# Second block of a two-block transformer on one core: 36 of 44 slabs of each large stage read normed, shifted rows; ScalarE evicts; modulation loads and small exchanges move to POOL's queue

## The chip, the cores and the metric

The kernel runs on one NeuronCore of one Trainium2 chip. Its engines work side by side: TensorE (PE) multiplies, and loads its weights in a stream of its own (PEld); VectorE (DVE), ScalarE (ACT) and GpSimd (POOL) compute on rows; SyncE (SP) issues DMA transfers, and so can ACT and POOL, each from its own queue. The 16 DMA engines are shared. Engines meet only at semaphores. The metric is the device time of one launch in microseconds (us): 1425.88 us is the median of three runs of the kernel before (1425.37 to 1426.09).

## The reference, cut to what matters

Input x has 256 tokens of width 1024. First come two hybrid layers (attention, mLSTM, MLP), which the change touches only through their DMA queues. Then two layers of the second block:

```python
mod = silu(c) @ w_ada[l] + b_ada[l]                       # (1024) x (1024, 6144)
sh1, sc1, g1, sh2, sc2, g2 = split(mod, 6)
h = rmsnorm(x, norm1[l]) * (1 + sc1) + sh1
proj = h @ w_in[l]                                        # (256, 1024) x (1024, 5632)
q, k, v, g_sw, p_in, gates = split(proj)                  # q, k: rotary; retention; pooling
merged = sigmoid(a_ret) * (... @ w_ret_o[l]) + sigmoid(a_pool) * (... @ w_pool_o[l])
x = x + g1 * (merged @ w_out[l])
h2 = rmsnorm(x, norm2[l]) * (1 + sc2) + sh2
gate, up = split(h2 @ w_ffn_in[l], 2)                     # (256, 1024) x (1024, 5632)
x = x + g2 * ((silu(gate) * up) @ w_ffn_out[l])
```

rmsnorm divides each token's row by its root mean square. The modulation vector mod is one matrix-vector product per layer, from 24 MB of weights.

## The kernel before, in words

**Slabs.** Every weight matrix is cut into slabs of 1024 x 128 values (512 KB), 450 in all. A slab passes through four steps, always in the same order: SP loads it into one of NS = 8 places of `raw`, once the slab eight before it has been used (`slab_used`); ACT copies it to `w_hi` (L583), rounded to the type that TensorE multiplies fast; DVE writes the rest, `w_lo` = raw - w_hi (L1082); PE multiplies. Activations are split in the same way, into a high and a low part. The function `slab` (L1938 to L1940) makes 24 matmuls of a slab: for each of its eight row tiles k, high by high, high by low and low by high. A slab's result, 128 features by 256 tokens, gathers in one of four banks of `acc`, so that a bank is written again four slabs later.

**Stages of the second block.** Slabs 190 to 319 are its first layer, 320 to 449 its second. In each: 44 slabs of w_in (I call it the projection stage), 8 of w_ret_o, 4 of w_pool_o, 8 of w_out, 44 of w_ffn_in, alternately gate and up (u counts the 22 pairs), and 22 of w_ffn_out. The first w_ffn_in slab of layer 0 is slab 254.

**The norm is folded in behind the matmul.** The rows `h2` that the projection and w_ffn_in stages multiply are x times the column gain, not yet divided by the root mean square, so that PE can start before that root is known. After the 256 token columns stand two more columns that hold the shift (high and low part); a matmul here therefore moves W = 258 columns. When a slab is done, DVE multiplies 258 columns of the bank by `rstd` (in `to_sbuf`, L1600, and for gate and up at L1874 and L1877; `rstd` has ones in its last columns), and the shift's product is added as a bias afterwards: by ACT in `shift` (L909) in the projection stage, within silu (L1052) and within the product of gate and up (L1881) in the other.

**Order of work.** It is written out by hand for each engine. `hi_upto(i)` and `lo_upto(i)` on ACT and DVE make all parts up to slab i. A queue is strictly in order: what stands behind a waiting instruction waits too.

**Modulation.** `load_ada` on SP loads `ada`, 96 pieces of 512 KB, into three places; DVE multiplies and adds them (`ada_product`, L1166 and L1172, two per piece), PE sums them (`ada_sums`, L1990) and DVE takes the columns (`ada_columns`). SP's queue holds these loads between those of the slabs; a load of `ada` waits for the place to be free (`ada_sum`), and the slab loads stand behind it.

**Rotary.** q and k are exchanged by halves of a head through SBUF-to-SBUF DMAs (`partners`, four DMAs of 64 KB each, into `rotb`), also on SP; `rope2` on DVE waits for them.

**The names in the order's rows.** `hn_x`, `hn_hi` and `hn_lo` are new semaphores: a pair of tiles of x times rstd is ready, a high tile is ready, a low pair is ready. `landed3` and the like are the landings of a raw place.

## Time and profile before

| | |
|---|---|
| median of 3 runs | 1425.88 us |
| the profiled execution, its own time | 1428.8 us |
| its span (first to last instruction) | 1426.1 us |
| mean granted TensorE clock | 0.996 |
| PE / PEld / DVE / ACT / POOL busy | 98 / 92 / 80 / 58 / 1 % |
| DMA queues | SP and its like 292.00 MB (72.9% of 16 engines' span); POOL's 1.66 MB |

Busy is a share of the span. All times of a trace count from the start of the span. A row of the timeline has start, duration, engine, line, operation, output<-inputs and shape; "x3" joins three instructions, and what stands in brackets is the idle time before it and what ended it. Instructions of one engine overlap a little: the step from one start to the next is shorter than the duration. In a row of the stretches, the numbers behind the length are the busy time of each engine with its count of instructions, then the granted TensorE clock (1.00 is 2.4 GHz, 0.50 is 1.2 GHz), the busy share of the DMA engines and GB/s.

### The profile page before, as it was taken

The numbers are of one execution on the slowest core, as the hardware profiler recorded it, in microseconds if no ns is written. First come the engines' busy times: TensorE is split into PE (matmuls) and PEld (weight loads), VectorE is DVE, ScalarE is ACT, GpSimd is POOL, SyncE is SP. The second block draws the span as 40 slices with busy tenths as digits, with TensorE's granted clock in tenths as the row PEclk, the third lists the DMA queues.
The fourth block names the chain that finished last, engine by engine and source line by source line (L and its number), as shares of the span: only waits on it lengthen the run. The fifth ranks groups of instructions, "written<-read, shape, count | busy, mean of one in ns | idle before, by whom it ended". The sixth has DMA issues, their size and how long they took to land.

```text
span 1426.1 us, 25528 instructions
## 1 busy us (share of the span) xinstructions
PE 1401.7 (98%) x10325; PEld 1312.9 (92%) x10325; DVE 1147.6 (80%) x1805; ACT 822.8 (58%) x1245; POOL 10.5 (1%) x21
## 2 busy tenths in 40 slices
PE   8999999999999999999999999999999999999997
PEld 8898888888888888889999999998999999999986
DVE  7898888888898888887778777777787887777763
ACT  6776776445776775344656555444446575644552
POOL 2000000000000000000000000000000000000000
PEclk9999999999999999999999999999999999999998
DMA  9544999986446999988754578898787556778661
GB/s 263 157 143 117 285 265 272 292 226 163 134 140 191 272 263 297 278 245 225 213 148 148 176 235 224 220 252 227 231 230 217 147 151 184 228 208 235 179 186 65
DMA packets 485363, 297.12 MB, mean 208 GB/s; under 512 B 14956, under 2 KB 455792, under 8 KB 485120
## 3 DMA queue, kind: packets, MB, share of 16 engines
q1 hardware_dynamic: 483728, 292.00, 72.9%
q8 instruction: 82, 1.34, 0.4%
q10 hardware_dynamic: 816, 1.84, 0.4%
q0 software_dynamic: 704, 1.66, 0.3%
q14 instruction: 33, 0.27, 0.1%
HBM read 289.43 MB, written 1.05 MB: 204 GB/s over the span
## 4 chain that ended last, share of the span: by engine, by line
PE 78%; DVE 13%; issue 3%; ACT 3%; DMA 2%; SPq 1%; DVEq 0%; ACTq 0%
PE acc L1938 15%; PE acc L1939 15%; PE acc L1940 14%; PE acc L1955 8%; PE mx L1955 6%; DVE w_lo L1082 5%; PE acc L1956 4%; PE mx L1956 3%; DVE ada_acc L1172 3%; ACT w_hi L583 1%; PE acc L1970 1%; PE acc L1972 1%; PE acc L1971 1%; DMA raw<-in_w_down 1%; DMA rotb<-projb 1%
## 5 line engine op out<-in xcount | busy, mean ns | idle before, releaser
L1082 DVE TENSOR_TENSOR w_lo<-raw,w_hi 128x1024 fp32r<-128x1024 f32 x450 | 541.6, 1221 | 111.2 <-ACT w_hi L583 109.4
L583 ACT ACTIVATE w_hi<-raw 128x1024 fp32r<-128x1024 f32 x450 | 458.0, 1049 | 135.5 <-DMA raw<-in_w_in 82.5
L1938 PE MATMUL acc<-h,w_hi 128*128 128x258 f32 (+1 forms) x1776 | 509.4, 287 | 7.6 <-DVE h L1109 2.8
L1939 PE MATMUL acc<-h,w_hi 128*128 128x258 f32 (+1 forms) x1776 | 503.8, 284 | 0.0
L1940 PE MATMUL acc<-h,w_lo 128*128 128x258 f32 (+1 forms) x1776 | 498.0, 280 | 0.0
L1938 PEld LDWEIGHTS acc<-h,w_hi 128*128 128x128 f32 x1776 | 334.4, 188 | 15.1 <-issue 4.7
L1940 PEld LDWEIGHTS acc<-h,w_lo 128*128 128x128 f32 x1776 | 338.5, 191 | 0.0
L1939 PEld LDWEIGHTS acc<-h,w_hi 128*128 128x128 f32 x1776 | 335.3, 189 | 2.6 <-issue 2.4
L1955 PE MATMUL mx<-u,w_hi 128*128 128x512 f32 x864 | 302.2, 392 | 0.0
L1956 PE MATMUL mx<-u,w_lo 128*128 128x256 f32 x864 | 243.6, 282 | 0.0
L1955 PEld LDWEIGHTS mx<-u,w_hi 128*128 128x128 f32 x864 | 162.2, 188 | 33.2
L1955 PE MATMUL acc<-h,w_hi 128*128 128x512 f32 x512 | 178.9, 392 | 1.1 <-issue 1.1
L1956 PEld LDWEIGHTS mx<-u,w_lo 128*128 128x128 f32 x864 | 163.6, 189 | 0.0
L1956 PE MATMUL acc<-h,w_lo 128*128 128x256 f32 x512 | 144.4, 282 | 0.0
L1172 DVE SCALAR_TENSOR_TENSOR ada_acc<-ada,cact,ada_acc 128x512 f32<-128x512 f32 x168 | 125.6, 748 | 2.6
L1955 PEld LDWEIGHTS acc<-h,w_hi 128*128 128x128 f32 x512 | 96.1, 188 | 21.5 <-issue 1.7
L1956 PEld LDWEIGHTS acc<-h,w_lo 128*128 128x128 f32 x512 | 96.9, 189 | 0.1
L1052 ACT ACTIVATE gt<-gt 128x256 f32<-128x256 f32 x44 | 22.4, 510 | 85.8 <-DVE gt L1874 85.8
L1938 PE MATMUL acc<-y,w_hi 128*128 128x256 f32 x224 | 63.0, 281 | 0.0
L1940 PE MATMUL acc<-y,w_lo 128*128 128x256 f32 x224 | 62.8, 280 | 0.0
L1939 PE MATMUL acc<-y,w_hi 128*128 128x256 f32 x224 | 62.5, 279 | 0.0
L608 ACT ACTIVATE h<-xT,nx 128x256 fp32r<-128x256 f32 x16 | 8.2, 510 | 74.7 <-DVE xT L1583 44.2
(294 smaller groups left out, 1642.8 us busy)
## 6 DMA issues: line engine op xcount, KB each, us to landing
raw<-in_w_in SPq DMA_DIRECT2D x132, 512.0 KB, 4.1
ada<-in_w_ada SPq DMA_DIRECT2D x96, 512.0 KB, 5.1
raw<-in_w_ffn_in SPq DMA_DIRECT2D x88, 512.0 KB, 4.6
raw<-in_w_up SPq DMA_DIRECT2D x64, 512.0 KB, 5.9
raw<-in_w_down SPq DMA_DIRECT2D x64, 512.0 KB, 6.5
raw<-in_w_out SPq DMA_DIRECT2D x32, 512.0 KB, 4.1
raw<-in_w_ffn_out SPq DMA_DIRECT2D x32, 512.0 KB, 4.2
raw<-in_w_ret_o SPq DMA_DIRECT2D x16, 512.0 KB, 4.1
```

Of the source, the lines that this page charges most:

```text
L583: nc.scalar.activation(w_hi[:, n % NS], raw[:, n % NS], ACT.Copy).then_inc(hi_ready, 1)
L1052: nc.scalar.activation(gt[:, u % 2, 0:S], gt[:, u % 2, 0:S], ACT.Silu, bias=gt[:, u % 2, S:W - 1]).then_inc(g_silu, 1)
L1082: V.tensor_tensor(w_lo[:, n % NS], raw[:, n % NS], w_hi[:, n % NS].bitcast(F32), ALU.subtract).then_inc(lo_ready, 1)
L1172: ins = V.scalar_tensor_tensor(o, ada[:, e % 3, part], w, o, ALU.mult, ALU.add)
L1938: mm(outp, w_hi[:, i % NS, k], rhs[:, k, 0], start=k == 0, stop=False)
L1939: mm(outp, w_hi[:, i % NS, k], rhs[:, k, 1], start=False, stop=False)
L1940: ins = mm(outp, w_lo[:, i % NS, k], rhs[:, k, 0], start=False, stop=k == KT - 1)
L1955: mm(halves(bank), w_hi[:, i % NS, j], part, start=first, stop=False)
L1956: return mm(bank[:, S:], w_lo[:, i % NS, j], part[:, 0], start=False, stop=last)
L1970: mm(o, w_hi[:, i % NS, n], hi, start=first and n % 2 == 0, stop=False)
L1971: mm(o, w_hi[:, i % NS, n], lo, start=False, stop=False)
L1972: return mm(o, w_lo[:, i % NS, n], hi, start=False, stop=last and n % 2 == 1)
```

## The change

1. From the ninth slab (FOLD = 8) of the projection stage and of the w_ffn_in stage on, in both layers, PE multiplies finished rows: x times rstd, times gain, plus shift. A matmul there moves 256 columns. Of 44 slabs 36 are changed in each of the four stages.
2. These rows are made beside the first eight slabs. DVE multiplies x by rstd, two tiles at a time (`scaled_pair`, four per stage, 128x512); ACT makes of each of the eight tiles a whole and a rounded copy (`normed_high`, two activations a tile); DVE takes the difference (`normed_low`, four per stage, 128x512). In the projection stage they stand in `y2` for slabs 8 to 12, and four DMAs of 512 KB on POOL's queue copy them into the place of `h2` (`hd2`) for slabs 13 (B_HOME) to 43, because `y2` is needed again. In the w_ffn_in stage they have a tile of their own, `h3`.
3. For the 36 slabs, ACT evicts the bank in one step: `place` (a copy) instead of DVE's `to_sbuf` and ACT's `shift`; silu reads gate from the bank; DVE's product of gate and up reads up from the bank.
4. All 96 `ada` loads go from SP's to POOL's queue, with a wait for the slab count that stood before them in SP's order. The exchanges of the second block (`partners`) go to POOL's queue too. `P_LOADS`, the slabs of the projection stage beside which eight of the loads stand, goes from 3 to 22 to 20 to 29, and the 16 products, two sums and two column steps of that stage move to later slabs.

The diff, cut to its core:

```diff
+FOLD = 8
+B_HOME = 13
-P_LOADS = (3, 4, 5, 12, 13, 16, 18, 22)
+P_LOADS = (20, 20, 20, 21, 23, 25, 27, 29)
 # POOL
+            def modulation(stage, i0, first, end):
+                for p, e in ada_loads(stage)[first:end]:
+                    pool.wait_ge(slab_used, i0 + p - NS + 1)
+                    if e >= 3:
+                        pool.wait_ge(ada_sum, e - 2)
...
+                    pool.dma_start(ada[:, e % 3], ...).then_inc(ada_landed[e % 3], 16)
+                partners(0)
+                partners(1)
+                pool.wait_ge(slab_used, b0[l] + FOLD)
+                for b in range(4):
+                    pool.wait_ge(hn_lo, 8 * l + b + 1)
+                    pool.dma_start(hd2[:, 2 * b:2 * b + 2], y2[:, 2 * b:2 * b + 2]).then_inc(h_home, 16)
+                partners(2)
+                partners(3)
+                pool.wait_ge(h_home, 64 * (l + 1))
+                modulation(("P", l), b0[l], 0, 8)
+                modulation(("F", l), b_ffn[l], 0, 4 * ADA_PLAN["F", l][1])
 # ACT
+            def normed_high(counts, n, k, whole, tile, gain, shift):
+                ready, high, low = counts
+                b = k // 2
+                act.wait_ge(ready, 4 * n + b + 1)
+                if b >= 2:
+                    act.wait_ge(low, 4 * n + b - 1)
+                nc.scalar.activation(whole[b % 2][:, k % 2], sqt[:, b % 2, k % 2], ACT.Identity, scale=gain(k), bias=shift(k))
+                nc.scalar.activation(tile[:, k, 0], sqt[:, b % 2, k % 2], ACT.Identity, scale=gain(k), bias=shift(k)).then_inc(high, 1)
+                def place(*chunks):
+                    for i in chunks:
+                        act.wait_ge(slab_used, p0 + i + 1)
+                        nc.scalar.activation(projb[:, i, 0:S], acc[:, i % 4, 0:S], ACT.Copy).then_inc(bp_sh, 1)
...
                 for u in range(22):
                     at = f0 + 2 * u
                     hi_upto(at + AHEAD)
+                    if u < FOLD // 2:
...
+                    else:
+                        act.wait_ge(slab_used, at + 1)
+                        nc.scalar.activation(gt[:, u % 2, 0:S], acc[:, 2 * u % 4, 0:S], ACT.Silu).then_inc(g_silu, 1)
+                    if u < 3:
+                        whole_tiles(3 * u, 3 * u + 1)
                     hi_upto(at + AHEAD + 2)
+                    if u < 2:
+                        whole_tiles(3 * u + 2)
                     act.wait_ge(g_prod, l * 22 + u + 1)
 # DVE
+            def scaled_pair(counts, n, b):
+                ready, high, _ = counts
+                if b >= 2:
+                    dve.wait_ge(high, 8 * n + 2 * b - 2)
+                V.tensor_tensor(sqt[:, b % 2], xT[:, 2 * b:2 * b + 2], rstd[:, 0:S]..., ALU.mult).then_inc(ready, 1)
+            def normed_low(counts, n, b, whole, tile):
+                _, high, low = counts
+                dve.wait_ge(high, 8 * n + 2 * b + 2)
+                V.tensor_tensor(tile[:, 2 * b:2 * b + 2, 1], whole[b % 2], tile[:, 2 * b:2 * b + 2, 0]..., ALU.subtract).then_inc(low, 1)
 # PE
+                        if i >= FOLD:
+                            if i == B_HOME:
+                                pe.wait_ge(h_home, 64 * (l + 1))
+                            slab(p0 + i, y2 if i < B_HOME else hd2, acc[:, i % 4, 0:S],
+                                 before=(lambda k: pe.wait_ge(hn_lo, 8 * l + k // 2 + 1)) if i == FOLD else None).then_inc(slab_used, 1)
+                    if s >= FOLD:
+                        slab(f0 + s, h3, acc[:, s % 4, 0:S],
+                             before=(lambda t: pe.wait_ge(hn_lo, (2 * l + 1) * 4 + t // 2 + 1)) if s == FOLD else None).then_inc(slab_used, 1)
```

**DVE at the start of the w_ffn_in stage.** The rows below are DVE's in the kernel before, from the end of the root to the product of the third pair's step. gt and upv are gate and up, L1887 is the low part of their product.

```order
L1089 SCALAR_TENSOR_TENSOR rstd<-rs_tmp,rstd 128x256 [waits chain_n]
L1874 TENSOR_TENSOR gt<-acc,rstd 128x258 [waits slab_used,chain_n]
L1082 TENSOR_TENSOR w_lo<-raw,w_hi 128x1024 [waits hi_ready] x3
L1877 TENSOR_TENSOR upv<-acc,rstd 128x258 [waits slab_used]
L1082 TENSOR_TENSOR w_lo<-raw,w_hi 128x1024 [waits hi_ready]
L1881 SCALAR_TENSOR_TENSOR upv<-upv,gt 128x256 [waits g_silu,g_up]
L1082 TENSOR_TENSOR w_lo<-raw,w_hi 128x1024 [waits hi_ready]
L1887 TENSOR_TENSOR u<-upv,u 128x256 [waits g_hi]
L1874 TENSOR_TENSOR gt<-acc,rstd 128x258 [waits slab_used]
L1877 TENSOR_TENSOR upv<-acc,rstd 128x258 [waits slab_used]
L1082 TENSOR_TENSOR w_lo<-raw,w_hi 128x1024 [waits hi_ready]
```

In the changed kernel the same place begins so (L1273 is `scaled_pair`, L1280 `normed_low`; L1156 is w_lo, L1960 gate, L1967 up):

```order
L1163 SCALAR_TENSOR_TENSOR rstd<-rs_tmp,rstd 128x256 [waits chain_n]
L1273 TENSOR_TENSOR sqt<-xT,rstd 128x512 [waits chain_n]
L1273 TENSOR_TENSOR sqt<-xT,rstd 128x512
L1960 TENSOR_TENSOR gt<-acc,rstd 128x258 [waits slab_used]
L1156 TENSOR_TENSOR w_lo<-raw,w_hi 128x1024 [waits hi_ready] x3
L1967 TENSOR_TENSOR upv<-acc,rstd 128x258 [waits slab_used]
L1156 TENSOR_TENSOR w_lo<-raw,w_hi 128x1024 [waits hi_ready]
L1972 SCALAR_TENSOR_TENSOR upv<-upv,gt 128x256 [waits g_up,g_silu]
L1280 TENSOR_TENSOR h<-f_whole,h 128x2x256 [waits hn_hi]
L1273 TENSOR_TENSOR sqt<-xT,rstd 128x512 [waits hn_hi]
L1156 TENSOR_TENSOR w_lo<-raw,w_hi 128x1024 [waits hi_ready]
L1988 TENSOR_TENSOR u<-upv,u 128x256 [waits g_hi]
```

Two steps stand ahead of the first gate and so ahead of the three w_lo behind it, two more behind the first product. The third pair's part of the same order is this; PE's ninth slab reads what its L1280, the fourth, writes:

```order
L1960 TENSOR_TENSOR gt<-acc,rstd 128x258 [waits slab_used]
L1967 TENSOR_TENSOR upv<-acc,rstd 128x258 [waits slab_used]
L1156 TENSOR_TENSOR w_lo<-raw,w_hi 128x1024 [waits hi_ready]
L1972 SCALAR_TENSOR_TENSOR upv<-upv,gt 128x256 [waits g_up,g_silu]
L1280 TENSOR_TENSOR h<-f_whole,h 128x2x256 [waits hn_hi]
```

The fourth low pair stands behind the w_lo of the eleventh slab and the third product.

**ACT at the same place.** Before, from the table load on (L1052 is silu, L1055 the high part of the product):

```order
L1047 ACT_TABLE_LOAD
L583 ACTIVATE w_hi<-raw 128x1024 [waits landed3]
L1052 ACTIVATE gt<-gt 128x256 [waits g_scaled]
L583 ACTIVATE w_hi<-raw 128x1024 [waits landed4]
L583 ACTIVATE w_hi<-raw 128x1024 [waits landed5]
L1055 ACTIVATE u<-upv 128x256 [waits g_prod]
```

In the changed kernel the third pair's part on ACT is this (L633 and L634 are `normed_high`, L1119 silu, L587 w_hi):

```order
L1119 ACTIVATE gt<-gt 128x256 [waits g_scaled]
L633 ACTIVATE f_whole<-sqt,modT,nx 128x256 [waits hn_lo,hn_x]
L634 ACTIVATE h<-sqt,modT,nx 128x256
L633 ACTIVATE f_whole<-sqt,modT,nx 128x256 [waits hn_lo,hn_x]
L634 ACTIVATE h<-sqt,modT,nx 128x256
L587 ACTIVATE w_hi<-raw 128x1024 [waits landed0]
L587 ACTIVATE w_hi<-raw 128x1024 [waits landed1]
```

Four activations stand between silu and the two w_hi. The first and the second pair have four there as well, and two more behind the w_hi; before there was none.

**POOL's queue in the projection stage of a layer,** which held nothing there before:

```order
L563 DMA rotb<-projb 32x2x256 [waits bp_sh]
L563 DMA rotb<-projb 32x2x256 x3
L570 DMA h<-y 128x1024 [waits hn_lo,slab_used]
L570 DMA h<-y 128x1024 [waits hn_lo] x3
L563 DMA rotb<-projb 32x2x256 [waits b_rope,bp_sh]
L563 DMA rotb<-projb 32x2x256 x3
L539 DMA ada<-in_w_ada 128x2x512 [waits ada_sum,slab_used,h_home]
```

What stood between the slab loads on SP (L440 and L433 before) stands here, and SP's projection stage is 44 slab loads in a row.

## Rows read from the trace of the kernel before

**Rows 1.** The page: busy time, share of the span, instructions.
```profile
PE 1401.7 (98%) x10325; PEld 1312.9 (92%) x10325; DVE 1147.6 (80%) x1805; ACT 822.8 (58%) x1245; POOL 10.5 (1%) x21
```

**Rows 2.** Stretches of whole slabs: six w_ret_o, six w_out, eleven w_ffn_in, three projection.
```profile
780.98:797.78 16.80, 16.80 (x146) 16.80 (x145) 12.96 (x20) 11.16 (x13) 0.00 (x0) 1.00 0.54 172
817.60:834.56 16.96, 16.96 (x146) 16.96 (x145) 13.85 (x26) 10.56 (x20) 0.00 (x0) 1.00 0.74 208
858.39:890.00 31.61, 31.61 (x267) 31.61 (x265) 24.87 (x40) 15.18 (x22) 0.00 (x0) 1.00 0.86 233
645.28:653.90 8.62, 8.62 (x75) 8.62 (x73) 4.86 (x8) 2.92 (x4) 0.00 (x0) 1.00 0.84 248
```

**Rows 3.** Stretches with a wait: projection slabs 201 and 202, then 331 and 332.
```profile
662.52:671.91 9.39, 7.54 (x51) 7.33 (x50) 9.32 (x14) 1.32 (x2) 0.00 (x0) 0.82 0.70 185
665.00:670.00 5.00, 3.15 (x19) 2.94 (x18) 5.00 (x9) 0.00 (x0) 0.00 (x0) 0.79 0.56 145
1056.70:1062.86 6.16, 6.02 (x50) 5.81 (x49) 6.13 (x10) 0.98 (x2) 0.00 (x0) 1.00 0.68 195
```

**Rows 4.** Timeline, projection stage of layer 0: DVE, ACT and PE.
```profile
657.81 0.69 DVE L1606 TENSOR_TENSOR rotb<-rotb,con 128x512 f32<-128x512 f32 x1 [6.16 <-DMA rotb<-projb]
658.42 0.69 DVE L1607 TENSOR_TENSOR projb<-projb,con 128x512 f32<-128x512 f32 x1
660.25 1.70 ACT L909 ACTIVATE projb<-projb 128x256 f32<-128x256 f32 x4
667.41 0.39 PE L1938 MATMUL acc<-h,w_hi 128*128 128x258 f32 x1 [1.85 <-DVE projb L1600]
```

**Rows 5.** Timeline, DVE, start of the w_ffn_in stage of layer 0.
```profile
841.77 0.43 DVE L1089 SCALAR_TENSOR_TENSOR rstd<-rs_tmp,rstd 128x256 f32<-128x256 f32 x1
842.23 0.43 DVE L1874 TENSOR_TENSOR gt<-acc,rstd 128x258 f32<-128x258 f32 x1
842.57 3.49 DVE L1082 TENSOR_TENSOR w_lo<-raw,w_hi 128x1024 fp32r<-128x1024 f32 x3
845.98 0.42 DVE L1877 TENSOR_TENSOR upv<-acc,rstd 128x258 f32<-128x258 f32 x1
...
847.45 0.48 DVE L1881 SCALAR_TENSOR_TENSOR upv<-upv,gt 128x256 f32<-128x256 f32 x1
847.84 1.22 DVE L1082 TENSOR_TENSOR w_lo<-raw,w_hi 128x1024 fp32r<-128x1024 f32 x1
...
849.31 0.42 DVE L1874 TENSOR_TENSOR gt<-acc,rstd 128x258 f32<-128x258 f32 x1
849.65 0.42 DVE L1877 TENSOR_TENSOR upv<-acc,rstd 128x258 f32<-128x258 f32 x1
```

**Rows 6.** Timeline, ACT, start of the w_ffn_in stage of layer 0.
```profile
842.13 1.06 ACT L583 ACTIVATE w_hi<-raw 128x1024 fp32r<-128x1024 f32 x1
843.10 0.49 ACT L1052 ACTIVATE gt<-gt 128x256 f32<-128x256 f32 x1
```

**Rows 7.** Stretch of the third w_ffn_in slab of layer 0, slab 256.
```profile
840.75:843.93 3.18, 3.04 (x26) 2.85 (x25) 2.98 (x6) 3.15 (x5) 0.00 (x0) 1.00 0.97 320
```

**Rows 8.** Timeline, DVE, first step behind the root, projection stage of layer 0.
```profile
639.83 0.48 DVE L1166 TENSOR_SCALAR ada_acc<-ada,cact 128x512 f32<-128x512 f32 x1
```

**Rows 9.** DMA issues: output<-input, queue, count, KB each, median us to landing.
```profile
ada<-in_w_ada SPq DMA_DIRECT2D x96, 512.0 KB, 5.1
con<-consts POOLq DMA_DIRECT2D x1, 1056.0 KB, 8.0
wgrp<-in_w_pool_grp POOLq DMA_DIRECT2D x1, 512.0 KB, 6.3
rows<-in_ln ACTq DMA_DIRECT2D x2, 8.0 KB, 2.1
rows<-in_b_ada POOLq DMA_DIRECT2D x1, 48.0 KB, 5.1
```

**Rows 10.** Timeline: an ada load's issue, and the first DVE step that reads it.
```profile
233.05 0.37 SPq L433 DMA_DIRECT2D ada<-in_w_ada  x1
241.98 1.53 DVE L1172 SCALAR_TENSOR_TENSOR ada_acc<-ada,cact,ada_acc 128x512 f32<-128x512 f32 x2
```

More of the change, by code:

```diff
@@ new lines, in _ @@
+                shift(2)
+                hi_upto(p0 + 9)
+                shift(3)
+                whole_tiles(4, 5)
+                hi_upto(p0 + 10)
+                shift(4)
+                whole_tiles(6, 7)
+                hi_upto(p0 + 11)
+                shift(5)
+                hi_upto(p0 + 12)
+                shift(6)
+                hi_upto(p0 + 13)
+                shift(7)
+                hi_upto(p0 + 14)
+                for i in range(FOLD, 18):
+                    place(i)
+                    hi_upto(p0 + i + 7)
@@ L965, in _ @@
                 values(0)
-                shift(13, 14, 15)
+                place(18)
+                hi_upto(p0 + 25)
+                place(19)
                 hi_upto(p0 + 26)
-                shift(16, 17, 18)
+                values(1)
+                place(20)
                 hi_upto(p0 + 27)
-                shift(19)
+                place(21)
                 hi_upto(p0 + 28)
-                values(1)
                 values(2)
+                place(22)
+                hi_upto(p0 + 29)
@@ L985, in _ @@
+                hi_upto(p0 + 34)
+                place(28)
+                hi_upto(p0 + 35)
+                place(29)
                 hi_upto(p0 + 36)
+                place(30)
+                hi_upto(p0 + 37)
                 squares(1)
+                place(31)
+                hi_upto(p0 + 38)
                 gated_high(0)
                 roots(1)
-                hi_upto(p0 + 37)
+                place(32)
+                hi_upto(p0 + 39)
+                place(33)
+                hi_upto(p0 + 40)
@@ L990, in _ @@
                 gated_high(1)
-                shift(28)
-                hi_upto(p0 + 39)
+                place(34)
+                hi_upto(p0 + 41)
+                values(3)
                 squares(2)
-                values(3)
+                place(35)
+                hi_upto(p0 + 42)
                 roots(2)
-                hi_upto(p0 + 40)
-                shift(29, 30)
-                hi_upto(p0 + 41)
+                place(36)
+                hi_upto(p0 + 43)
+                place(37)
@@ L999, in _ @@
+                hi_upto(p0 + 44)
                 gated_high(2)
-                hi_upto(p0 + 43)
+                place(38)
+                hi_upto(p0 + 45)
                 squares(3)
-                shift(31, 32, 33, 34)
+                place(39)
+                hi_upto(p0 + 46)
                 roots(3)
-                hi_upto(p0 + 46)
-                shift(35, 36)
+                place(40)
+                hi_upto(p0 + 47)
+                place(41)
+                hi_upto(p0 + 48)
@@ L1006, in _ @@
                 gated_high(3)
[L1007 removed]
+                place(42)
                 hi_upto(p0 + 49)
[L1009 to L1011 removed]
                 branch_gate(0)
[L1013 to L1016 removed]
+                place(43)
+                hi_upto(p0 + 52)
                 branch_gate(1)
@@ L1047, in _, with whole_tiles @@
                 nc.scalar.preload_act_table(ACT.Silu)
+                def whole_tiles(*tiles):
+                    for k in tiles:
+                        normed_high(h_norm, (2 * l + 1), k, (f_whole[:, 0], f_whole[:, 1]), h3, nx2_of(l), lambda k: mod_of(l, 3 * KT + k))
                 for u in range(22):
@@ L1709, in _ @@
                 norm_root(l * 2 + 4)
+                scaled_pair(h_norm, 2 * l, 0)
+                scaled_pair(h_norm, 2 * l, 1)
+                to_sbuf(0, 1)
+                lo_upto(p0 + 7)
+                whole_low(0)
+                scaled_pair(h_norm, 2 * l, 2)
+                to_sbuf(2)
+                lo_upto(p0 + 8)
+                to_sbuf(3)
+                whole_low(1)
+                scaled_pair(h_norm, 2 * l, 3)
+                lo_upto(p0 + 9)
+                to_sbuf(4)
@@ L1710, in _ @@
+                whole_low(2)
+                lo_upto(p0 + 10)
+                to_sbuf(5)
+                lo_upto(p0 + 11)
+                whole_low(3)
+                to_sbuf(6)
+                lo_upto(p0 + 12)
+                rope2(0)
+                to_sbuf(7)
+                lo_upto(p0 + 14)
+                rope2(1)
+                lo_upto(p0 + 16)
+                rope2(2)
+                lo_upto(p0 + 17)
+                rope2(3)
+                lo_upto(p0 + 19)
                 ada_product(8 * g0 + 0)
-                to_sbuf(0, 1, 2)
```

281 lines of the change are left out of this document (130 added, 151 removed).

## Prediction

> **What bounds the kernel now.** I read the page's first part, then stretches cut at the starts of slabs, then the timeline where a stretch is longer than its neighbours. The page says that PE is busy 98% of the span and the rest far less [rows 1], so a microsecond leaves the span only if PE's own work shrinks or one of its few waits goes, and every new wait of PE adds itself in full. The stretches give the price of PE's work. Six w_ret_o slabs (256 columns) take 16.80 us, 2.800 each; six w_out slabs, the same code and tiles, 16.96, 2.827 each; eleven w_ffn_in slabs (258 columns) 31.61, and three projection slabs 8.62, both 2.873 each [rows 2]. The waits left in the second block are small but for one: slabs 201 and 202 take 9.39 us instead of 5.75, because a projection slab waited 1.85 us for DVE's eviction of a bank [rows 3, 4]. DVE was late because it had stood 6.16 us at the first rotary step for its exchange, with evictions behind it [rows 4]. From 665 to 670 us the granted clock is 0.79 in the mean: right behind that wait PE ran at 1.2 instead of 2.4 GHz for a while [rows 3]. In layer 1 the same two slabs take 6.16 us, 0.41 too many [rows 3].
>
> **The change, part by part.**
>
> *Columns.* 36 slabs in each of four stages, 144, lose two columns per matmul. Against 2.873 a slab is worth 0.073 us by the w_ret_o row and 0.046 by the w_out row. I can't tell in which of the two rhythms the new slabs fall, so I take the middle, 0.060: 144 x 0.060 = 8.6 us gained, with ends of 6.6 and 10.5. That is 1.9 to 3.1 ns per matmul. The Trainium skill (TensorE: Matmul & The Clock Gate, "Wait — 56ns, not 53.3ns?") puts warm matmuls N / 2.4 GHz plus about 2.5 ns apart, which makes two columns worth 0.83 ns and all 3456 matmuls an estimated 2.9 us; by these rows the trace does not agree.
>
> *The exchange.* It moves off SP, and the first rotary step moves behind 12 slabs' w_lo; the evictions that stood behind it are gone from slab 8 on. So the waits at slabs 201, 202 and 331, 332 go: 9.39 - 5.75 = 3.64, and 0.41; 4.1 us gained. What is late next there is the new tiles. DVE's first free moment behind the root is 639.83 [rows 8]. By its order eight steps of 128x512 (0.61 from start to start [rows 4]), five evictions at 0.34 and five w_lo at 1.14 [rows 5], with the waits for ACT's 16 activations at 0.40 each ((1.70 - 0.50) / 3 [rows 4]) between its w_hi, put the fourth low pair at 654.7. PE's ninth slab starts at 653.9 [rows 2] and asks for it at its seventh tile, 6 x 0.35 = 2.1 us later, at 656.0: 1.3 us to spare, no wait.
>
> *Eviction on ACT.* `place` costs ACT what `shift` did (about 0.4), and DVE loses 36 evictions of 0.34 a stage. ACT's w_hi of slab j+7 now stands behind the eviction of slab j: 0.4 + 1.0 for ACT and 1.2 for DVE behind the end of slab j, against six slabs of 2.8 until PE needs it, 14 us to spare. No gain either, since DVE's time there is hidden behind PE. Later in the stage PE asks for two modulation sums, the retention weights and the gated products. Walked with the same steps, the closest is the third retention output: its gated product is done at about 739, PE is there at about 740. I put no cost, but that is thin.
>
> *The start of w_ffn_in.* Here, unlike in the projection stage, DVE and ACT have no lead. In the kernel before, the third slab already takes 3.18 us, 0.31 too many, since the fourth slab's w_lo ends at 843.8 (842.57 + 1.22) [rows 5, 7]. Walk it in the new order, layer 0.
> - Two `scaled_pair` at 842.23 push gate to 843.45 and the w_lo from 842.57 to 843.79; the first of these, for PE's fourth slab, is there at 845.0 instead of 843.8. PE waits 1.1 us more.
> - Then up 847.2, w_lo 847.6, product 848.7, the first low pair and the third scaled pair (two times 0.61) to 850.3, w_lo to 851.4, low part to 851.8, second gate to 852.1. Before it was at 849.31 [rows 5].
> - The second low pair needs tile 3, which ACT makes behind the second silu: 852.2 + 0.4 + 0.8, so DVE stands until 853.5. Third low pair at 857.05, w_lo, low part, third gate at 859.14.
> - ACT's third silu can start at 859.6; tiles 6 and 7 are four activations, to 861.6; w_hi of the eleventh slab (1.06 [rows 6]) until 862.7; DVE's w_lo behind it to 863.8, the third product 0.4, the fourth low pair, done 864.9.
> - PE's fourth slab starts at 845.05, the ninth five times 2.873 later, and it needs the third gate's eviction (859.14 + 0.43): 859.6, where it was 858.39. It asks for the fourth pair at its seventh tile, 861.7, and stands 3.2 us.
>
> Against the kernel before, where the seventh tile came at 858.39 + 6 x 0.36 = 860.5, the delay is 4.4 us in layer 0. Layer 1 has the same order, so 8.9 us in all. Each step's size is from a row, but eleven handovers are in it; I give it 3.4 to 5.4 per layer.
>
> *The clock.* A wait of 1.85 us was followed by the low clock; slab 202, 4.50 us, lost 1.6 by it (in the 9.39). A wait of 3.2 us should be followed by it too, in part while PE stands. I take 1.2 per layer, 2.4; bounds 0 and 3.4.
>
> *Home copies.* Four DMAs of 512 KB, issued from 653.9 (slab 8 begins) and 654.7 (fourth pair) on; PE's slab 13 wants them all at 653.9 + 5 x 2.8 = 667.9. No row has an SBUF-to-SBUF copy of this size. The nearest are POOL's loads: 6.3 us for 512 KB, 8.0 for 1056 KB, issue to landing [rows 9]. If they overlap fully they are home at about 662; as two loads of 8.0 in a row at about 670. I take no wait, since one DMA's latency overlaps the next, and keep the other end as a rival. The exchanges for pairs 2 and 3 stand behind them on POOL; only DVE's later rotary steps wait for these.
>
> *Modulation on POOL.* SP's slab loads no longer stand behind `ada`'s waits: hidden, nothing gained, since PE waits for no slab there. The loads have 241.98 - 233.05 = 8.9 us from issue to first use at the tightest place that I found [rows 10], and land in 5.1 from SP [rows 9]. Small loads at the start landed in 2.1 us from ACT's queue and 5.1 from POOL's [rows 9]; three more is 8.1, still inside. The Trainium skill (DMA: Bandwidth & Descriptors, "SWDGE vs HWDGE vs iDMA") says that the descriptors of POOL's DMAs are written into SBUF by POOL's own cores, which DVE can lock out in some of its modes, and that SP's are immune to this; it speaks for a longer tail.
>
> **Sum.** -8.6 - 4.1 + 8.9 + 2.4 = -1.4 us. The profiled execution's own time is 1428.8, so 1427.4; it stood 2.9 over the median of the runs, so the median comes to 1424.5.
>
> **Rivals.**
> 1. *The w_ffn_in start is no wait.* For it: ACT is busy only 58% and DVE 80% [rows 1], and if the handovers overlap more than I have them, the ninth slab finds its rows. Against: both walk in strict order, and the kernel before waits there already. Without the 3.2 us and the clock, with the 1.1 of the fourth slab left: -8.6 - 4.1 + 2.2 = -10.5, 1415.4.
> 2. *The home copies are late* (slower). One mechanism: 2 MB through 16 DMA engines that are 84% busy in the stretch just before [rows 2]. It decides once the copies need over 11 us from the last issue. As two loads of 8.0 us they come 2.2 us late, and with the low clock behind it (1.6) that is 3.8 per layer, 7.6: 1432.1. Against: twice the bytes took 8.0 us, not 12.6 [rows 9], so most of a DMA's time is not its data.
> 3. *Two columns are worth only themselves,* 2 / 2.4 GHz = 0.83 ns, and the rest of the difference between the stages comes from something else, such as which tiles PE reads there: 3456 x 0.83 ns = 2.9 us gained instead of 8.6, so 1430.2. The Trainium skill's rule above is this one. Against: four rows of 256 and 258 columns with no overlap [rows 2].
> 4. *POOL's loads of `ada` are late.* DVE stands at a product and w_lo behind it. It decides where a landing takes over 8.9 us plus w_lo's own lead. If one in five of the 24 groups of products cost PE 1 us, that is 4.8: 1429.3.
>
> **How the numbers follow.** My forecast has 0.60, rival 1 0.17, rival 2 0.12, rival 3 0.06, rival 4 0.05. 0.2% is 2.85 us, about what a measurement of this kernel can tell from no change: faster is below 1423.0, slower above 1428.7. The forecast's own range is 1421 to 1428; 0.27 of it lies below 1423.0 (columns at 10.5, or a clock that stays up) and 0.03 above 1428.7. Faster: 0.60 x 0.27 + 0.17 + 0.01 = 0.34. Slower: 0.02 + 0.12 + 0.05 + 0.02 = 0.21. No change: 0.45. The range goes from rival 1 to rival 2, 1415.5 to 1432.
>
> **What the new profile would show.** Stretches of the changed slabs at 2.80 or 2.83 us each; DVE's first rotary step without an idle time of 6 us and no wait near 665; a wait of PE of about 3 us for DVE's low pair (L1280) in the ninth w_ffn_in slab of both layers, with a granted clock under 1.00 behind it; 1 us more at the fourth slab; no wait of PE for the home copies. I am wrong if PE does not stand at that pair, if it stands at slab 13, or if new slabs take 2.87.

## The result, and the profile after

The changed kernel took 1431.33 us (median of 14 runs, 1427.75 to 1435.50); the kernel before, on the same chip and in turn with it, 1425.62 (14 runs, 1423.90 to 1431.95). The ratio is 1.0042, 95% interval [1.0029, 1.0054]: slower by 5.7 us, twice what a measurement of this kernel can tell from no change. The forecast was 1424.5, no change. The profiled execution took 1431.4 us, with a span of 1429.6 (before 1428.8 and 1426.1). The slower of the changed kernel's 14 runs had the lower mean granted clock: 0.992 or 0.993 in the four above 1433.7 us, 0.995 to 0.997 in the four below 1430.

The page of the changed kernel, beside [rows 1]:

```profile
PE 1395.1 (98%) x10325; PEld 1305.1 (91%) x10325; DVE 1120.2 (78%) x1693; ACT 847.0 (59%) x1309; POOL 101.6 (7%) x157
```

PE has 6.6 us less work and yet ends 3.5 us later in the span, so it stands idle 10 us more. Where it stands is in the table of what PE waited for, from slab 190 on (engine, tile and line, the releaser, then us in total, times, longest):

```profile
PE acc L2039 <- DVE h L1280: 6.7, 2, 3.4
PE mx L2496 <- ACT sqb L949: 3.5, 2, 2.0
PE acc L2039 <- DVE w_lo L1156: 2.7, 2, 1.4
...
PE acc L2039 <- DVE gt L1960: 0.8, 2, 0.4
PE acc L2039 <- DVE y L1280: 0.4, 2, 0.2
```

The first and third rows are the start of w_ffn_in, as forecast; the fourth is the ninth slab there, which waits for the third gate's eviction. The second row was not forecast: in `ret_sums(0)` PE sums the squares of the first retention output, and it waits for ACT, which makes them. The last row is the first folded projection slab (I call the 36 slabs of a stage that read the new rows folded).

Stretches of the changed kernel (columns as in [rows 2]): six folded projection slabs, six folded w_ffn_in slabs, the place of the old wait, then slabs nine and ten of w_ffn_in in layer 0 and in layer 1.

```profile
654.74:671.53 16.79, 16.79 (x146) 16.79 (x145) 12.86 (x16) 7.64 (x13) 6.50 (x11) 1.00 1.13 309
876.55:893.35 16.80, 16.80 (x146) 16.80 (x145) 11.62 (x16) 9.29 (x13) 1.45 (x2) 1.00 0.83 236
665.00:670.00 5.00, 5.00 (x45) 5.00 (x44) 3.69 (x5) 2.01 (x4) 2.33 (x4) 1.00 1.20 252
854.45:860.99 6.54, 3.18 (x24) 2.98 (x25) 3.37 (x6) 4.78 (x8) 0.00 (x0) 1.00 0.28 81
860.99:865.35 4.36, 4.36 (x26) 4.36 (x25) 3.17 (x6) 2.41 (x3) 0.00 (x0) 0.61 0.43 124
1249.48:1256.66 7.18, 3.82 (x24) 3.62 (x25) 4.01 (x7) 4.78 (x8) 0.00 (x0) 0.82 0.27 75
1256.66:1261.37 4.71, 4.71 (x26) 4.71 (x26) 3.52 (x6) 3.63 (x6) 0.00 (x0) 0.56 0.39 111
```

A folded slab takes 2.80 us here, as the w_ret_o slabs of [rows 2] did; some of the projection stages take 2.83. The old wait is gone and the clock is 1.00 there, against 0.79 in [rows 3]. The ninth w_ffn_in slab takes 6.54 and 7.18 us instead of 2.87, and the tenth, without any wait, 4.36 and 4.71, at a granted clock of 0.61 and 0.56: PE was at 1.2 GHz for most of it.

Setting the starts of the same slabs of both traces side by side gives the account, in us of the span (minus is earlier):

| stretch | forecast | measured |
|---|---|---|
| up to the second block's ninth slab | 0 | -2.4 |
| projection stages, from the ninth slab (layer 0, layer 1) | -8.4 | -3.3, -0.4 |
| w_ffn_in to the end of the layer (layer 0, layer 1) | +7.0 | +4.4, +5.4 |
| all, with -0.3 behind the last slab | -1.4 | +3.5 |

From the second block's ninth slab on, the first that the new rows touch, the changed kernel thus loses 5.9 us (3.5 + 2.4), close to the 5.7 by which the medians differ. The 2.4 ahead of it is taken up in the last section.

The new wait in the projection stage, layer 0. First ACT (start, duration, and in brackets the idle time before with its releaser), then PE:

```profile
699.69 0.37 ACT L932 ACTIVATE projb<-acc 128x256 f32<-128x256 f32 x1
703.67 1.06 ACT L587 ACTIVATE w_hi<-raw 128x1024 fp32r<-128x1024 f32 x1 [3.61 <-DMA raw<-in_w_in]
704.75 1.28 ACT L964 ACT_TABLE_LOAD   x1
706.05 1.92 ACT L964 ACTIVATE projb<-projb 128x2048 f32<-128x2048 f32 x1
707.98 1.28 ACT L1024 ACT_TABLE_LOAD   x1
...
711.71 0.60 ACT L949 ACTIVATE sqb<-mx 128x512 f32<-128x512 f32 x1
```
```profile
712.46 1.10 PE L2496 MATMUL mx<-sqb,con 128*128 128x512 f32 x2 [1.95 <-ACT sqb L949]
```

ACT stands 3.6 us for a slab's load, with the silu and its two table loads behind that w_hi; two evictions and two w_hi follow before the squares. The kernel before had the squares right behind the second table load:

```profile
714.57 1.28 ACT L978 ACT_TABLE_LOAD   x1
715.86 0.60 ACT L919 ACTIVATE sqb<-mx 128x512 f32<-128x512 f32 x1
```

The start of w_ffn_in, layer 0, from the third unit on: DVE, then ACT.

```profile
851.89 0.69 DVE L1280 TENSOR_TENSOR h<-f_whole,h 128x512 fp32r<-128x512 f32 x1 [0.32 <-ACT h L634]
...
853.97 0.42 DVE L1960 TENSOR_TENSOR gt<-acc,rstd 128x258 f32<-128x258 f32 x1
...
857.90 1.23 DVE L1156 TENSOR_TENSOR w_lo<-raw,w_hi 128x1024 fp32r<-128x1024 f32 x1 [3.17 <-ACT w_hi L587]
859.04 0.48 DVE L1972 SCALAR_TENSOR_TENSOR upv<-upv,gt 128x256 f32<-128x256 f32 x1
859.44 0.69 DVE L1280 TENSOR_TENSOR h<-f_whole,h 128x512 fp32r<-128x512 f32 x1
```
```profile
854.43 0.51 ACT L1119 ACTIVATE gt<-gt 128x256 f32<-128x256 f32 x1 [2.26 <-DVE gt L1960]
854.85 0.59 ACT L633 ACTIVATE f_whole<-sqt,modT,nx 128x256 f32<-128x256 f32 x1
855.34 0.59 ACT L634 ACTIVATE h<-sqt,modT,nx 128x256 fp32r<-128x256 f32 x1
...
856.82 1.99 ACT L587 ACTIVATE w_hi<-raw 128x1024 fp32r<-128x1024 f32 x2
```

This is the chain that I had walked: gate, silu, four tile activations, a w_hi, DVE's w_lo, the product, the fourth pair. One activation follows another by 0.49 us (854.85 to 855.34), where I had taken 0.40.

### The profile page after: what moved, and what is told of

Same layout as the page of the kernel before. It is cut to its first block, busy times and chain, and to the rows that moved or that the text cites. A ratio compares the mean times of both kernels' runs of the same rounds, so it can differ in the third digit from the quotient of the medians.

```text
span 1429.6 us, 25595 instructions
## 1 busy us (share of the span) xinstructions
PE 1395.1 (98%) x10325; PEld 1305.1 (91%) x10325; DVE 1120.2 (78%) x1693; ACT 847.0 (59%) x1309; POOL 101.6 (7%) x157
## 4 chain that ended last, share of the span: by engine, by line
PE 75%; DVE 13%; ACT 7%; issue 3%; DMA 2%; DVEq 0%; ACTq 0%
PE acc L2039 14%; PE acc L2041 13%; PE acc L2040 13%; PE acc L2056 8%; PE mx L2056 6%; DVE w_lo L1156 5%; PE acc L2057 4%; PE mx L2057 3%; ACT w_hi L587 2%; DVE ada_acc L1246 2%; PE acc L2071 1%; PE acc L2072 1%; PE acc L2073 1%; DMA raw<-in_w_in 1%; PE acc L2177 1%
## 5 line engine op out<-in xcount | busy, mean ns | idle before, releaser
L1156 DVE TENSOR_TENSOR w_lo<-raw,w_hi 128x1024 fp32r<-128x1024 f32 x450 | 543.3, 1221 | 139.0 <-ACT w_hi L587 137.0
L587 ACT ACTIVATE w_hi<-raw 128x1024 fp32r<-128x1024 f32 x450 | 463.7, 1053 | 131.2 <-DMA raw<-in_w_in 65.2
L2039 PE MATMUL acc<-h,w_hi 128*128 128x256 f32 (+1 forms) x1696 | 486.3, 287 | 14.8 <-DVE h L1280 6.7
L2040 PE MATMUL acc<-h,w_hi 128*128 128x256 f32 (+1 forms) x1696 | 476.7, 281 | 0.0
L2041 PE MATMUL acc<-h,w_lo 128*128 128x256 f32 (+1 forms) x1696 | 475.1, 280 | 0.0
L2039 PEld LDWEIGHTS acc<-h,w_hi 128*128 128x128 f32 x1696 | 320.7, 189 | 22.7 <-issue 7.1
L2040 PEld LDWEIGHTS acc<-h,w_hi 128*128 128x128 f32 x1696 | 321.0, 189 | 2.6 <-issue 2.4
L2041 PEld LDWEIGHTS acc<-h,w_lo 128*128 128x128 f32 x1696 | 321.5, 190 | 0.0
L539 POOL DMA_DIRECT2D ada<-in_w_ada x96 | 69.5, 724 | 1010.4 <-DVE ada_acc L1246 362.4
L1246 DVE SCALAR_TENSOR_TENSOR ada_acc<-ada,cact,ada_acc 128x512 f32<-128x512 f32 x168 | 125.6, 748 | 2.5
L2056 PEld LDWEIGHTS acc<-h,w_hi 128*128 128x128 f32 x512 | 96.1, 188 | 21.6 <-issue 1.7
L2057 PEld LDWEIGHTS acc<-h,w_lo 128*128 128x128 f32 x512 | 96.8, 189 | 0.1
L2039 PE MATMUL acc<-y,w_hi 128*128 128x256 f32 x304 | 85.5, 281 | 0.4 <-DVE y L1280 0.4
L2041 PE MATMUL acc<-y,w_lo 128*128 128x256 f32 x304 | 85.0, 280 | 0.0
L2040 PE MATMUL acc<-y,w_hi 128*128 128x256 f32 x304 | 84.7, 279 | 0.0
L2039 PEld LDWEIGHTS acc<-y,w_hi 128*128 128x128 f32 x304 | 57.1, 188 | 0.8 <-DVE y L1280 0.8
```

The costliest lines, as they stand in the source:

```text
L539: pool.dma_start(ada[:, e % 3], ada_v[:, l * KT + 2 * part:l * KT + 2 * part + 2, at:at + ADA_GROUP]).then_inc(ada_landed[e % 3], 16)
L587: nc.scalar.activation(w_hi[:, n % NS], raw[:, n % NS], ACT.Copy).then_inc(hi_ready, 1)
L1156: V.tensor_tensor(w_lo[:, n % NS], raw[:, n % NS], w_hi[:, n % NS].bitcast(F32), ALU.subtract).then_inc(lo_ready, 1)
L1246: ins = V.scalar_tensor_tensor(o, ada[:, e % 3, part], w, o, ALU.mult, ALU.add)
L2039: mm(outp, w_hi[:, i % NS, k], rhs[:, k, 0], start=k == 0, stop=False)
L2040: mm(outp, w_hi[:, i % NS, k], rhs[:, k, 1], start=False, stop=False)
```

## The experiments

Each kernel was timed in turns with the kernel before on its own chip (1425.3 to 1426.3 there). The theories: **A**, PE's new waits and the clock behind them, set by the order of the steps; **B**, too little room on ACT and DVE, in whatever order; **C**, POOL's queue; **D** to **G** are named where they are tested.

**squares_first.**

```diff
                 gate_silu()
                 nc.scalar.preload_act_table_set(LOG_EXP)
+                squares(0)
                 place(24)
 ...
                 hi_upto(p0 + 32)
-                squares(0)
                 place(26)
```

> The changed kernel with one step moved: ACT's squares of the first retention pair stand right behind the table load that follows the silu, and no longer behind two evictions and two w_hi. Theory A (the cost is the place of this step in ACT's order): PE's two waits for the squares, 2.2 and 1.9 us in the changed kernel, go, and nothing else moves: 1431.3 - 3.9 = 1427.4 us, 1.001 of the kernel before. Theory B (ACT has too much work there, not a bad order): the three evictions and w_hi behind it come 0.6 us later, PE waits for one of them instead, and the time stays within 1 us of 1431.

1426.8 us, ratio 1.0008 [0.9998, 1.0018]. By the starts of slabs the projection stages take 2.2 and 1.4 us less than in the changed kernel (a wait of 0.3 us stays in layer 1), and PE waits for nothing else there. A, not B. Not all of the 4.5 us between the medians is shown to be the squares: in the traces another 1.2 lie at slab 393, the tenth w_ffn_in slab of layer 1, which the edit doesn't touch and which took 3.48 us here and 4.71 in the changed kernel, by the clock.

**ffn_unfolded.** `FOLD_F = 44` in w_ffn_in; its scaled_pair, whole_tiles and whole_low steps are left out.

> The changed kernel with the new tiles left out in w_ffn_in alone: all 44 slabs there read 258 columns, as before, and the projection stage keeps the change. Theory A (what the change loses is PE's waits at the start of w_ffn_in and the low clock behind them): by the starts of slabs in the two traces these are worth 6.9 us in layer 0 and 7.9 in layer 1; against them stand the columns of the folded slabs behind, 2 x 34 x 0.073 = 5.0. So 14.8 - 5.0 = 9.9 us faster than the changed kernel: 1421.5 us, 0.997 of the kernel before. Theory C (the loss comes from the loads on POOL's queue and its exchanges, which slow the kernel everywhere): only the columns are lost, 1431.3 + 5.0 = 1436 us, 1.007.

1423.0 us, 0.9980 [0.9971, 0.9989]: 8.3 us less than the changed kernel had. The sign and most of the size are A's; C would have given 1436. The fold of w_ffn_in cost more than the rest of the change brings.

**before_pool_ada.** `load_ada` and its calls are taken off SP, and POOL gets the `modulation` steps of the change.

> The kernel before with one edit of the change alone: the modulation weights are loaded from POOL's queue instead of SP's, each behind the use of the slab that it was queued behind on SP. Theory A (the queue is no cost): up to the second block the changed kernel is ahead of the one before by 2.1 us in the traces, and this edit is all that differs there: 1425.6 - 2.1 = 1423.5 us, 0.9985, with DVE's waits for the weights no longer than before. Theory C (POOL's loads land late and slow DVE's products, and PE by them): slower than before by 3 us or more, 1428.6 or above.

1425.3 us, 0.9996 [0.9986, 1.0005]: no difference that can be measured. C is out, and so is my rival 4; in the changed kernel's trace, too, no wait of DVE is for a load of `ada`. But its profiled execution took 1424.3 us, 4.5 less than that of the kernel before. See the section on what was not expected.

**pe_filler.**

```diff
+                def ninth(t):
+                    for _ in range(28 if t == 6 else 0):
+                        mm(mx[:, 3, 0:S], w_hi[:, (f0 + FOLD) % NS, 0], h2[:, 0, 0, 0:S], start=True, stop=True)
+                    pe.wait_ge(hn_lo, (2 * l + 1) * 4 + t // 2 + 1)
```

> The changed kernel, with 28 matmuls of 256 columns into a bank that nobody reads, put in front of the seventh tile of the ninth w_ffn_in slab in both layers. PE works there (28 x 0.117 = 3.3 us) instead of standing for the fourth low pair; the pair is as late as before. Theory A (the low clock behind the wait is due to PE's standing): the ninth and tenth slab no longer lose 1.7 us in layer 0 and 2.8 in layer 1 beside the wait itself, granted clock 1.00 there, and the time is 1431.3 - 4.5 = 1427 us, 1.001 of the kernel before. Theory D (the low clock comes with this stretch, whatever PE does in it): slabs nine and ten stay as long as they were, 1431 us.

1426.9 us, 1.0016 [1.0007, 1.0025]. Slabs nine and ten of layer 0, in its trace:

```profile
853.60:860.13 6.53, 6.46 (x52) 6.25 (x53) 3.37 (x6) 4.78 (x8) 0.00 (x0) 1.00 0.28 84
860.13:862.93 2.80, 2.80 (x26) 2.80 (x25) 1.67 (x4) 1.43 (x3) 0.00 (x0) 1.00 0.48 140
```

The ninth slab ends no earlier, since the pair is as late as before, but the tenth takes 2.80 instead of 4.36 and the clock stays at 1.00. So the low clock came from PE's standing; theory D falls. Slabs nine and ten together take 9.33 us in either layer here, and 10.90 and 11.89 in the changed kernel: the clock was worth 1.6 and 2.6, 4.1 us in all. The medians differ by 4.5.

**ffn_spread12.**

```diff
-                scaled_pair(h_norm, (2 * l + 1), 0)
-                scaled_pair(h_norm, (2 * l + 1), 1)
 ...                                   # DVE, behind the product of unit u
+                    if 1 <= u <= 4:
+                        whole_low(u - 1)
+                    if u < 4:
+                        scaled_pair(h_norm, (2 * l + 1), u)
 ...                                   # ACT, behind u_hi of unit u
+                    if u < 4:
+                        whole_tiles(2 * u, 2 * u + 1)
```

> The changed kernel with the tiles of w_ffn_in made one pair a unit (a unit is a gate and an up slab) in units 0 to 3, behind ACT's w_hi and u_hi and behind DVE's product, nothing of them ahead of the first gate, and read from slab 12 on. The arithmetic is the same. Theory A: PE finds the tiles ready, no wait over 0.5 us is left there and the clock stays up; the eight slabs more that read 258 columns cost 0.6: 1431.3 - 14.8 + 0.6 = 1417 us, 0.994 of the kernel before. Theory B (ACT and DVE have no room for 8 and 4.8 us of tiles within 12 slabs, in whichever order): they fall behind slab by slab, PE waits for w_lo or for a gate from slab 6 on, and at least half of the 14.8 stays: 1424 us or more.

1421.7 us, 0.9970 [0.9961, 0.9980]. The waits at slabs eight and nine are gone and that at slab four is as small as in the kernel before, but at the thirteenth slab, the first folded one, PE still stands for the last pair:

```profile
867.23 0.39 PE L2031 MATMUL acc<-h,w_hi 128*128 128x256 f32 x1 [1.38 <-DVE h L1280]
```

Two thirds of the gain that A promised came. B is right in that the tiles take longer than twelve slabs, and wrong in that they fit nowhere, which the next run shows.

**mended16.** ffn_spread12 with three edits more:

```diff
-FOLD_F = 12
+FOLD_F = 16
 ...                                   # ACT, projection stage
-                hi_upto(p0 + 30)
                 gate_silu()
                 nc.scalar.preload_act_table_set(LOG_EXP)
+                hi_upto(p0 + 30)
                 place(24)
+                squares(0)
                 hi_upto(p0 + 31)
 ...                                   # DVE, projection stage
+                whole_low(3)
                 lo_upto(p0 + 11)
-                whole_low(3)
```

> The spread tiles of w_ffn_in again, now read from slab 16 on, and in the projection stage two moves in ACT's order (gate_silu ahead of the w_hi that waits for its load, the squares of the first pair ahead of the next w_hi) and one in DVE's (the fourth low pair ahead of a w_lo). Theory A: of the spread12 run 1.7 us of wait per layer at slab 12 and the slow slab behind it go (1.9 and 1.6 us by the lengths of its slabs, less 0.6 for eight more slabs of 258 columns), as do the waits for the squares (3 us) and 0.4 per layer at the first folded projection slab: 1421.7 - 2.9 - 3.0 - 0.8 = 1415 us, 0.992 of the kernel before. Theory B (no room on ACT): the wait moves on to another slab, 1420 us or more.

1414.9 us, 0.9929 [0.9917, 0.9942]: the fastest, 16.4 less than the change as given. ACT in its trace, at the place shown above:

```profile
698.90 0.37 ACT L934 ACTIVATE projb<-acc 128x256 f32<-128x256 f32 x1
699.29 1.28 ACT L966 ACT_TABLE_LOAD   x1
700.58 1.92 ACT L966 ACTIVATE projb<-projb 128x2048 f32<-128x2048 f32 x1
702.52 1.28 ACT L1025 ACT_TABLE_LOAD   x1
703.82 1.06 ACT L589 ACTIVATE w_hi<-raw 128x1024 fp32r<-128x1024 f32 x1
704.78 0.36 ACT L934 ACTIVATE projb<-acc 128x256 f32<-128x256 f32 x1
705.52 0.60 ACT L951 ACTIVATE sqb<-mx 128x512 f32<-128x512 f32 x1 [0.37 <-PE mx L2477]
```

The table loads now fill the time in which ACT had stood for the load, and the squares start 6.2 us earlier, in a kernel that is 1.2 us ahead at this slab. What is left at the start of w_ffn_in is a wait of 1.0 us for a gate's eviction in layer 0, and a few of 0.2.

**columns_priced** and **before_256**, for my rival 3 (here theory E). The first puts a block in front of one slab of the kernel before; the second changes both slab calls of the second block:

```diff
+                    for n in (256, 258, 260, 262, 264, 272, 288, 258, 256) if k == 0 else ():
+                        for j in range(48):
+                            mm(mx[:, 3, 0:n], w_hi[:, (f0 + 20) % NS, j % KT], row[:, 0:n], start=True, stop=True)
```
```diff
-                    slab(f0 + s, h2, acc[:, s % 4, 0:W],
+                    slab(f0 + s, h2[:, :, :, 0:S], acc[:, s % 4, 0:S],
```

> The kernel before with a block of 9 x 48 matmuls in front of one w_ffn_in slab of layer 0, each with other weights than the one ahead of it, of 256, 258, 260, 262, 264, 272, 288, 258 and 256 columns; their result isn't read. It prices columns alone, with no wait and no other engine. Theory A (the difference of the stages is the columns): 258 is 3 ns longer from start to start than 256 (119.7 against 116.7), and the rows for 260 to 288 tell whether a column counts by itself or the chip rounds up. Theory E (rival 3: two columns cost 0.83 ns, the rest is which tiles PE reads): 258 is under 1.5 ns longer than 256.

> The kernel before with the two columns of the shift left out of all 88 slabs of the projection and of w_ffn_in in both layers; evictions, tiles and order are as before, and the shift is left out of the result. Theory A: 176 x 0.070 = 12.3 us faster, 1413.5 us, 0.991 of the kernel before, with slabs of 2.80 or 2.83 us. Theory E (two columns are worth 0.83 ns): 4224 x 0.83 ns = 3.5 us, 1422 us.

The block, 48 matmuls each of 256, 258 and 288 columns:

```profile
890.34:895.95 5.61, 5.61 (x50) 5.61 (x49) 4.38 (x8) 2.83 (x4) 0.00 (x0) 1.00 0.88 237
895.95:901.70 5.75, 5.75 (x50) 5.75 (x49) 1.87 (x3) 0.00 (x0) 0.00 (x0) 1.00 0.17 42
...
925.12:931.53 6.41, 6.41 (x51) 6.41 (x50) 0.00 (x0) 0.00 (x0) 0.00 (x0) 1.00 0.00 0
```

From start to start that is 116.9, 119.8 and 133.5 ns; 260, 262, 264 and 272 columns took 120.1, 120.0, 122.1 and 125.6. So 3 ns lie between 256 and 258, for A. But before_256 took 1422.9 us, 0.9982 [0.9973, 0.9991]: 2.4 us, not 12.3, as E has it. Six of its w_ffn_in slabs:

```profile
874.45:891.69 17.24, 17.24 (x146) 17.24 (x145) 13.66 (x23) 8.56 (x13) 0.00 (x0) 1.00 0.79 211
```

They take 2.873 us each, with 256 columns (others 2.85). Neither theory covers both runs, so a third: **F**, it counts where the moving row starts.

**starts_priced.**

```diff
+                    cases = [lambda j, o=o: row[:, o:o + S] for o in (0, 2, 4, 8, 16, 32, 64)]
+                    cases += [lambda j: h2[:, j % KT, 0, 0:S], lambda j: h2[:, j % KT, j % 2, 0:S], lambda j: h2[:, j % KT, j % 2]]
+                    cases += [lambda j: hd2[:, j % KT, 0], lambda j: hd2[:, j % KT, j % 2]]
```

> The kernel before with a block of 12 x 48 matmuls in front of one w_ffn_in slab of layer 0; their result isn't read. Seven cases read the same 256 columns' length from one row of h2, from element 0, 2, 4, 8, 16, 32 and 64 on; two read h2's rows of 258 elements in turn, 256 columns of each (one with the high rows alone, one with high and low); one reads 258 columns of them; two read the same memory as packed rows of 256 elements. Theory F (a row of 256 columns is quick only where it starts on a boundary of SBUF, which the 258-element rows of h2 mostly miss and the rows of the new tiles never): packed rows and the aligned starts 116.7 ns from start to start, the other starts and h2's rows of 256 columns 118.5 to 119.7. Theory A (columns alone): every case of 256 columns 116.7, and only the one of 258 columns 119.7.

256 columns from element 0, 2 and 64 of a row; h2's rows, high and low in turn; packed rows, the high ones alone (high and low in turn took the same, 116.7 ns):

```profile
891.42:897.03 5.61, 5.61 (x50) 5.61 (x49) 4.38 (x8) 2.83 (x4) 0.00 (x0) 1.00 0.87 239
897.03:902.78 5.75, 5.75 (x51) 5.75 (x50) 1.87 (x3) 0.00 (x0) 0.00 (x0) 1.00 0.16 40
...
925.50:931.10 5.60, 5.60 (x50) 5.60 (x49) 0.00 (x0) 0.00 (x0) 0.00 (x0) 1.00 0.00 0
...
936.78:942.47 5.69, 5.69 (x50) 5.69 (x49) 0.00 (x0) 0.00 (x0) 0.00 (x0) 1.00 0.00 0
...
948.26:953.86 5.60, 5.60 (x51) 5.60 (x49) 0.00 (x0) 0.00 (x0) 0.00 (x0) 1.00 0.01 3
```

116.9, 119.7, 116.8, 118.5 and 116.7 ns; from element 4, 8, 16 and 32 it is 118.3, 117.8, 120.0 and 117.3. And 258 columns of h2's rows in turn took 120.6, 0.7 more than from element 0 of one row. F: of the starts tried, those a multiple of 64 elements (256 bytes) from the tile's start are the quick ones.

**before_256_wide** and **before_wide.** h2's rows 272 elements apart, with 256 and with 258 columns computed.

> The kernel before with 256 columns in all 88 slabs of the projection and of w_ffn_in in both layers, as in before_256 (the shift is left out of the result), and with h2's rows 272 elements apart instead of 258. Theory F: each slab takes 2.80 us in place of the 2.85 to 2.87 that 256 columns took out of rows 258 apart: 176 x 0.070 = 12.3 us off the kernel before, 1413 us, 0.991. Theory G (the stages differ by something else than columns and row starts, such as what DVE and ACT do beside PE): no faster than before_256, 1422 us, 0.998.

> The kernel before with one edit: h2's rows are 272 elements apart instead of 258; 258 columns are computed, and the result is the same. Theory F: 258 columns out of an aligned row take what they take now (119.9 ns in the priced block against 119.7 in the slabs), so no change, 1425.5 us, 1.000. If the row starts cost something of their own to 258 columns too, it is faster by up to 176 x 24 x 1 ns = 4 us, 0.997.

1423.4 us, 0.9980 [0.9969, 0.9990], and 1428.4 us, 1.0019 [1.0008, 1.0030]. Both expectations failed, and by my choice of the distance: 272 is no multiple of 64, and y2 behind h2 moved by 896 bytes. Six slabs of w_ffn_in took 16.96 us in the first; six w_ret_o slabs, which read y2 and are not edited, took 17.09 in the second, where [rows 2] has 16.80:

```profile
781.70:798.79 17.09, 17.09 (x147) 17.09 (x145) 12.92 (x20) 11.35 (x13) 0.00 (x0) 1.00 0.58 178
```

**before_256_packed**, the same test with rows 256 elements apart in the same memory:

```diff
+        h2_all = sb("h2", [P, KT * 2 * W], F32R)
+        h2 = h2_all[:, 0:KT * 2 * S].rearrange("p (k a s) -> p k a s", k=KT, a=2)
+        h_cols = h2_all[:, KT * 2 * S:].rearrange("p (k a s) -> p k a s", k=KT, a=2)
```

> The kernel before with 256 columns in all 88 slabs of the projection and of w_ffn_in, as in before_256 (the shift is left out of the result), and with h2's rows packed, 256 elements apart, in the same memory; the shift columns are written behind the last row and not read. Theory F (start of the row and columns together): the packed rows of the priced block took 116.7 ns where rows 258 apart took 118.5, so each slab takes 2.80 us: 176 x 0.070 = 12.3 us off the kernel before, 1413 us, 0.991. Theory G (the stages differ by something else than columns and row starts): as before_256 and before_256_wide, 1423 us, 0.998.

```profile
872.80:889.60 16.80, 16.80 (x147) 16.80 (x145) 13.22 (x23) 8.49 (x12) 0.00 (x0) 1.00 0.89 230
```

Six slabs in 16.80 us, and 1417.8 us, 0.9937 [0.9921, 0.9952]. Slabs took 2.80 in w_ffn_in, 2.80 or 2.83 in the projection. F holds and G falls. The time gained 8.2 of the 12.3 us; the profiled execution has 4.0 of the rest in one place: slabs 300 and 301, in w_ffn_out of layer 0, took 6.12 and 3.90 us instead of 3.13 and 2.87, a wait of 2.2 us for DVE's low part of u and the low clock behind it (0.71 in slab 301). That execution is the slowest of the six, 3.6 us over the median, so whether the others had this wait is open.

## Why the prediction was wrong, step by step

- **Eviction on ACT: "I put no cost, but that is thin."** This step failed. I had named three groups of consumers (modulation sums, retention weights, gated products) and not the squares, which ACT itself makes and PE waits for. With their order changed, ACT did them behind two more evictions and two w_hi. PE stood 1.95 and 1.6 us. Slabs 216 to 222 of layer 0 and their like in layer 1 lost 2.2 and 1.8, once two columns a slab and the modulation sums that now stand there (0.44) are taken off: 4.0 us where the sum has nothing. squares_first gave 3.6 of it back.
- **The fourth low pair of the projection stage, "1.3 us to spare, no wait".** This failed too: it was 0.2 us late, and the slab took 3.28 us instead of 2.80, 0.9 in both layers. Sixteen activations at 0.49 instead of 0.40, 1.4 us more, take the 1.3 away.
- **The start of w_ffn_in, +8.9, and the clock, +2.4.** The mechanism was right: fourth slab +1.21 (forecast 1.1), ninth slab standing 3.4 us at its seventh tile (forecast 3.2), low clock behind. The sizes were too small: the third gate is 0.56 later than I had it, the last pair 0.9. Together the layers lost 6.9 and 7.9 us, 14.8 for 11.3, and 4.1 of it is the clock, where I had 2.4 with a bound of 3.4.
- **The profiled execution's surplus is not where it went wrong.** Taking off 2.9 us only brings the sum back to the median before: the forecast is that median less 1.4. The medians differ by +5.7, and the traces by +5.9 from the ninth slab of the second block on. So the miss is in the terms: squares 4.0 for 0, w_ffn_in 14.8 for 11.3 and the fourth low pair 0.9 for 0, with the columns 1 us better than forecast.
- **Columns, -8.6.** Right in size, and a little small (2.80 us a slab in w_ffn_in, 2.80 or 2.83 in the projection stages, which makes about 9.8 by the slabs' lengths), for a reason of which half was missing. Two columns out of h2's rows are worth little (before_256: 2.4 us for 176 slabs); the gain needs the new tiles' packed rows too. Rival 3 had guessed this half: "which tiles PE reads there". The Trainium skill's rule (TensorE: Matmul & The Clock Gate, "Wait — 56ns, not 53.3ns?"), 0.83 ns for two columns, comes close for rows that stay 258 apart: 4224 x 0.83 = 3.5 us against 2.4 measured. It doesn't hold between packed 256 and 258 columns, 3 ns.
- **Right:** the projection wait is gone (-3.6 in layer 0 and -0.4 in layer 1, by the starts of slabs, without columns and moved sums); PE does not wait for home copies (7.1 us from issue to landing, median of eight) at slab 13; POOL's loads of `ada` (5.7 us) hold up nothing. Rivals 2 and 4 fall with that, rival 1 with the waits. But 1.6 of the 3.6 is the low clock behind the old wait, and that is not in every execution: see the last section.

## What to carry to other kernels

When the order on an engine is rewritten, list every product of that engine for which the bottleneck engine waits, those it makes for itself too, and walk each one: two evictions and two w_hi put in ahead of `squares(0)` cost 4 us here. A stand of PE of 3.4 us cost twice here, once for the wait and once for the slow clock behind it; it is worth pushing the first use four slabs on, at 0.07 us a slab, to lose it. And look at where the moving rows start before you count columns.
